# A decoder block on one core: the 512-column products read their moving operand by turns from its two halves

## What is computed

```
mod = c @ w_mod + b_mod; shift, scale, gate = split(mod, 3)
u = x * (1 + scale) + shift
q,k,v,z_a, cb,cc,cx,z_b, g_a,g_b = split(u @ w_in)          # 2048 x 12288
y_a = rmsnorm((softmax(q1 k1^T) - lam * softmax(q2 k2^T)) v) * silu(z_a)   # 8 heads, causal, rotary
y_b = cb * causal_conv3(cc * cx) * silu(z_b)
h = sigmoid(g_a) * (y_a @ w_proj_a) + sigmoid(g_b) * (y_b @ w_proj_b)
out = layernorm(alpha * x + gate * (h @ w_out)) * ln_gain + ln_bias
```

## Time and profile before

| | |
|---|---|
| median of 3 runs | 1563.55 us (1563.29 to 1564.33) |
| profiled execution | 1565.23 us, its span 1563.5 us |
| PE busy | 1498.8 us, 6600 instructions |
| DVE busy | 819.4 us |
| ACT busy | 501.1 us |
| POOL busy | 44.0 us |
| granted TensorE clock, mean | 0.991 of full speed |

### The profile page before, as it was taken

The page is one execution under the profiler, slowest core; times in us unless marked ns, Lnnn a source line. Parts: engine busy times, 40 slices in busy tenths (PEclk is TensorE's granted clock), DMA queues, the critical chain, the costliest instruction groups (busy, mean ns, idle before and its releaser), DMA issues.

```text
span 1563.5 us, 18079 instructions
## 1 busy us (share of the span) xinstructions
PE 1498.8 (96%) x6600; PEld 1220.2 (78%) x6600; DVE 819.4 (52%) x1072; ACT 501.1 (32%) x693; POOL 44.0 (3%) x52
## 2 busy tenths in 40 slices
PE   2889999999999999999999999999999999999994
PEld 2667788787887878878787888888788888888883
DVE  6997764647546375463754742222522323434448
ACT  1215434425344243443434422223122221422121
POOL 0000000000000000000000000000000000000004
PEclk9999999999999999999999999999999999999997
DMA  9995432533324334233433232322232232362312
GB/s 346 382 382 155 135 108 69 147 107 107 108 85 130 107 111 123 82 114 107 132 110 94 82 135 80 107 93 96 82 107 98 90 107 80 108 254 96 107 54 108
DMA packets 215248, 200.22 MB, mean 128 GB/s; under 512 B 7729, under 2 KB 176433, under 8 KB 214449
## 3 DMA queue, kind: packets, MB, share of 16 engines
q1 hardware_dynamic: 209648, 176.52, 34.9%
q0 software_dynamic: 4608, 16.78, 3.9%
q10 hardware_dynamic: 962, 6.53, 1.0%
HBM read 195.61 MB, written 4.19 MB: 128 GB/s over the span
## 4 chain that ended last, share of the span: by engine, by line
PE 88%; DVE 7%; issue 2%; ACT 1%; DMA 1%; SPq 0%; POOLq 0%; POOL 0%; ACTq 0%; DVEq 0%
PE acc L992 28%; PE acc L993 28%; PE acc L994 28%; DVE mod_sum L631 2%; PE sc L1081 2%; DVE w_lo L604 1%; PE misc L1099 1%; DMA w_mod_in<-in_w_mod 1%; PE sc L1090 1%; DVE res L975 1%; DVE res L951 0%; ACT act_hi L431 0%; DVE gate L653 0%; PE misc L1041 0%; DVE act_lo L658 0%
## 5 line engine op out<-in xcount | busy, mean ns | idle before, releaser
L604 DVE TENSOR_TENSOR w_lo<-raw,w_hi 128x1024 fp32r<-128x1024 f32 (+1 forms) x258 | 310.6, 1215 | 599.6 <-ACT w_hi L388 599.5
L992 PE MATMUL acc<-act_hi,w_hi 128*128 128x512 f32 x1472 | 579.2, 394 | 21.8 <-DVE w_lo L604 13.9
L994 PE MATMUL acc<-act_hi,w_lo 128*128 128x512 f32 x1472 | 574.8, 390 | 0.0
L993 PE MATMUL acc<-act_lo,w_hi 128*128 128x512 f32 x1472 | 574.3, 390 | 0.0
L388 ACT ACTIVATE w_hi<-raw 128x1024 fp32r<-128x1024 f32 (+1 forms) x258 | 268.9, 1052 | 720.0 <-PE acc L994 637.9
L992 PEld LDWEIGHTS acc<-act_hi,w_hi 128*128 128x128 f32 x1472 | 277.2, 188 | 93.6 <-issue 35.8
L994 PEld LDWEIGHTS acc<-act_hi,w_lo 128*128 128x128 f32 x1472 | 277.3, 188 | 58.6
L993 PEld LDWEIGHTS acc<-act_lo,w_hi 128*128 128x128 f32 x1472 | 277.5, 189 | 56.7 <-issue 0.2
L994 PE MATMUL acc<-y_hi,w_lo 128*128 128x512 f32 x256 | 99.6, 389 | 0.0
L992 PE MATMUL acc<-y_hi,w_hi 128*128 128x512 f32 x256 | 99.6, 389 | 0.0
L993 PE MATMUL acc<-y_lo,w_hi 128*128 128x512 f32 x256 | 99.6, 389 | 0.0
(11 more groups left out here) (151 smaller groups left out, 990.9 us busy)
## 6 DMA issues: line engine op xcount, KB each, us to landing
raw<-in_w_in SPq DMA_DIRECT2D x256, 256.0 KB
w_mod_in<-in_w_mod SPq DMA_DIRECT2D x64, 512.0 KB, 6.9
raw<-in_w_tail SPq DMA_DIRECT2D x32, 1024.0 KB
raw<-in_w_in SPq DMA_DIRECT2D x29, 1024.0 KB
gate_in<-in_w_mod POOLq DMA_DIRECT2D x32, 512.0 KB, 4.2
x_in<-in_xT SPq DMA_DIRECT2D x8, 512.0 KB, 8.0
x_tok<-in_x ACTq DMA_DIRECT2D x1, 4096.0 KB, 13.2
raw<-in_w_in SPq DMA_DIRECT2D x8, 384.0 KB
```

The lines of the kernel that those rows point to most:

```text
L604: ins = dve.tensor_tensor(w_lo[:, f % SLOTS, :, 0:width], raw[:, (f // 2) % 2, 2 * (f % 2):2 * (f % 2) + 2, 0:width], w_hi[:, f % SLOTS, : ...
L992: pe.matmul(dst, a_hi, b_hi, start=first, stop=False)
L993: pe.matmul(dst, a_hi, b_lo, start=False, stop=False)
L994: return pe.matmul(dst, a_lo, b_hi, start=False, stop=last)
```

## The change

`three` gives its output and its two moving operands a second shape before it issues its matmuls. The 512 elements of a partition are seen as two halves (`a`) of 16 runs (`l`) of 16 elements (`e`, `LINE`), and read in the order run 0 of the first half, run 0 of the second, run 1 of the first, and so on. The output is written in the same order, so that each column lands where it landed before. The stationary operand, the number of instructions, every wait and the other matmuls (L1041, L1069, L1081, L1090, L1099, L1104, L1105, L1134) are as they were.

```diff
@@ -58,6 +58,7 @@
 LEAD = 3
 SLOTS = 4
+LINE = 16
@@ -987,8 +988,13 @@
         @block.tensor
         def _(pe):
+            def two_runs(row):
+
+                return row.rearrange("p (a l e) -> p l a e", a=2, e=LINE)
+
             def three(dst, a_hi, a_lo, b_hi, b_lo, first, last):

+                dst, b_hi, b_lo = two_runs(dst), two_runs(b_hi), two_runs(b_lo)
                 pe.matmul(dst, a_hi, b_hi, start=first, stop=False)
                 pe.matmul(dst, a_hi, b_lo, start=False, stop=False)
                 return pe.matmul(dst, a_lo, b_hi, start=False, stop=last)
```

## The result

The changed kernel takes 1639.38 us (median of 4 runs, 1637.9 to 1640.69), before it is 1563.67 us (median of 4, 1563.29 to 1564.33). The ratio is 1.0483, with a 95% interval of 1.0465 to 1.0502: slower by 75.7 us. The profiled execution took 1637.9 us with a span of 1636.2 us, against 1565.23 and 1563.5 us before.

The account below looks back on a forecast made before the run. The prediction took TensorE's pace on the products of `three` from 150 us on as the bound. It added nothing to the median of the kernel before, giving 1563.5 us, with an 8-in-10 range of 1486 to 1600.

Parts of the forecast that it names:

- What bounds the kernel: From 150 us on, TensorE's pace on 5,796 products of `three`, 226.7 ns each, 1,314 us of the 1563.5 us span.
- What a product consists of: Product of `three`: 512 columns are 213.3 ns, measured 226.7; of 13.3 ns surplus, 3.3 is switch, about 10 the stream.
- I take nothing: Products of `three`: surplus is a fixed step per line, kept by the change; 226.7 ns stays, 1563.5 us, chance 0.36.
- The faster rival: Products of `three`: the two halves can be read ahead of each other, -58 us, 1505 us, end -77 us; chance 0.34.
- Weight load and stream out of step: Products of `three`: new address order never lets both reads settle, 4.6 ns more each, +27 us, 1590 us; chance 0.13.
- A jump costs: Moving operand or output of `three`: each jump costs a cycle or more, +77 us at one, 1641 us; chance 0.17.

Follow-up runs that it names:

- The widths: All but first and last row blocks of each bank stream 384 or 256 columns: contiguous 173.3 and 119.7 ns, 16-element runs by turns 180.0 and 120.0 ns per product.

## Why the prediction was wrong

The forecast was no change, 1563.5 us, with a range of 1486 to 1600. The measured 1639.4 lies outside it and on the slow side.

- **What bounds the kernel.** Right. TensorE's pace rules from 150 us on, and one nanosecond on each of the 5,796 products is 5.8 us: 13.3 ns by that lever are 77.3 us, measured 75.7. Part of the rest is that products near the mean of squares were above 226.7 ns already before.
- **What a product consists of.** This is the step that failed. "Of the 13.3 ns too many, about 10 then belong to a stream that takes an element in every cycle" was concluded from float32 products at two cycles per column, whose switch costs 3.3 ns. (The 3.3 ns come from the chain; the starts of the same eight products, 2.041 us for seven of them and 2,432 columns, give 2.0.) A small switch there was carried over to products at one cycle per column. The widths show that the part paid once per product is 32 cycles here, 13.3 ns, at 256, 384 and 512 columns, and that no part is paid per 16 elements. That 32 is also the number of 16-element steps in 512 columns was a coincidence, and the forecast stood on it. All rows of the trace of before had the same width at that pace, so they could not tell the two apart.
- **"I take nothing", since "the change keeps the number of steps".** Wrong for the same reason. There was no cost per line to be kept. Broken into runs of 16 by turns from two halves, the reading needs 18 cycles per run, 576 in all, where the contiguous product took 544; 32 cycles are new. By the model of the longer of two paces, the reading's other 32 surplus cycles lie where the 32 of the switch were. The prediction's support for this term, that "where a contiguous operand lies makes no difference", doesn't hold either: by the kernel's allocations all operands of the earlier trace rows and of the 443 products begin at a multiple of 64 bytes, and with one of them 32 bytes further on a product takes 233.3 ns.
- **The faster rival.** No order that was tried is faster than the contiguous one. Since the surplus is paid once per product, there was nothing for an order of lines to win.
- **Weight load and stream out of step.** Contiguous products that vary from one to the next around 230 ns do exist, and two experiments stay there: 230.0 ns with a narrower weight load and 233.3 ns with one operand 32 bytes further on. That two reads are then in each other's way is not shown. It isn't what the change did; its products are an even 240.0 ns apart.
- **A jump costs.** This rival came true, at the price worked out for it: 240.0 ns for "an even 240 ns or more", 1639.4 us for 1641. Its mechanism is only half right: the output's jumps are free, and the moving operand's cost two cycles for a run of 16, of which, by the model, one was covered. That one cycle per run comes out in the sum is luck of the length 16: at 32 and 8 it would give 233.3 and 253.3 ns, measured 236.7 and 243.3. It had 0.17 for everything beyond 1600, half of what the faster case had, though by the prediction's own words no row spoke against it; one outcome can't say more of that chance.
- **The range.** It ended between two rivals of about equal weight. Its top of 1600 left out the one case that had an exact price for a single cycle per run.

What stays open: why a run of 16 costs two cycles, and why four parts in turns with runs of 16 give 230.8 ns, less than the 240.0 of 18 cycles per run, when two parts, at any distance tried, give 240.0 and eight parts 239.6; what sets the pace below 16 elements (a product takes 584 cycles with runs of 8, 600 with 4, 816 with 2) and at 32, where it takes 568 cycles and neither pace alone explains it; and by what an operand 32 bytes further on slows the stream. Nor is it shown that the 32 cycles belong to the switch: every product measured has a weight load of its own (6600 of each), even the second of `three`, which has the same stationary operand as the first and comes at the same distance. A fixed cost of any product would look the same. Neighbours matter too: in the trace of the widths, the contiguous products of 512 columns that are left between narrower ones are 231 to 234 ns apart, and no model here has that. The longer of two paces fits contiguous operands and two parts with runs of 16 (within 1.7 ns), 24 at 480 columns, and 48 or more; elsewhere it fails or is untried.

## What to carry to other kernels

Where a stream of such float32r products is the bound, its moving operand is best read contiguously, or in runs of at least 64 elements, and the place of both operands in memory is worth a test: 32 bytes cost 39 us here. In this kernel the PSUM side could be broken up into runs of 16 at no cost. A surplus in a product's distance isn't assigned to the stream or to the switch until two widths have been measured, however well its number fits a count of steps. Where a rival has an exact price and nothing in the trace speaks against it, the range has to reach it.

## What the runs showed of the hardware

- A product of float32r with a weight load of its own takes its columns plus 32 cycles of 2.4 GHz from start to start: 119.7, 173.3 and 226.7 ns at 256, 384 and 512 columns. The page TensorE: Matmul & The Clock Gate of the Trainium skill (Wait — 56ns, not 53.3ns?) has about 2.5 ns as the fixed cost of a product at the full clock; these runs show 13.3 ns for float32r. Half or a quarter of the weight columns does not shorten it (230.0 and 231.6 ns at 512 columns).
- A moving operand in runs of 16 elements, by turns from two parts, takes 18 cycles per run (180.0 and 240.0 ns at 384 and 512 columns; 226.7 ns at 480, 1.7 ns more), and then no switch is to be seen. From four parts it takes less, 230.8 ns at 512 columns.
- Activation tiles (`act_hi`, `act_lo`) 32 bytes further on make the whole kernel 39 us slower, 1602.35 against 1563.24 us (one execution each): 233.3 ns per product, whether they move or stand.
